# Queries and keys of the mLSTM groups and of two attention groups turned by VectorE and through DRAM

## The reference, cut to what matters

```python
scores = einsum('cbhtd,cbhsd->cbhts', q, k)              # mLSTM, times exp(gate matrix), masked
h      = scores_gated @ v / max(|row sum|, exp(-m))
s      = einsum('bshd,bmhd->bhsm', q, mk) * Dh**-0.5     # attention to the memory
out    = softmax(s) @ mv                                 # and the same, with bias, in the band
```

## Time and profile before

| | us |
|---|---|
| median of 3 runs (2137.60 to 2139.51) | 2139.01 |
| the profiled execution, its own time | 2139.0 |
| its span, first to last instruction | 2137.4 |
| TensorE busy | 2118.9 |
| VectorE busy | 1312.0 |
| ScalarE busy | 1108.1 |
| mean granted clock of TensorE, share of full | 0.997 |

### The profile page before, as it was taken

One profiled execution on the slowest core, in us unless ns is written; L12 is line 12 of the kernel. 1 busy time (PEld: TensorE's weight loads), 2 busy tenths in 40 slices (PEclk: granted clock), 3 DMA queues, 4 the chain that ended last, 5 costly groups with the idle time before them and its releaser, 6 DMA issues.

```text
span 2137.4 us, 29849 instructions
## 1 busy us (share of the span) xinstructions
PE 2118.9 (99%) x10852; PEld 1753.3 (82%) x10852; DVE 1312.0 (61%) x1745; ACT 1108.1 (52%) x1468; POOL 156.2 (7%) x256
## 2 busy tenths in 40 slices
PE   9999999999999999999999999999999999999998
PEld 7888888888888787888878888888888788888886
DVE  6456556464553877787776565566546845567467
ACT  6554545454444848474755454445444544545453
POOL 7000000000000100000010000100001211000012
PEclk9999999999999999999999999999999999999999
DMA  9866566666565555454556765755658567555654
GB/s 337 269 182 214 172 213 195 199 198 217 179 206 184 148 157 169 143 173 139 177 144 220 254 185 170 226 146 170 193 181 302 181 204 193 167 162 182 200 178 159
DMA packets 211584, 411.00 MB, mean 192 GB/s; under 512 B 14096, under 2 KB 31009, under 8 KB 211070
## 3 DMA queue, kind: packets, MB, share of 16 engines
q1 hardware_dynamic: 199440, 369.94, 55.7%
q0 software_dynamic: 9712, 30.98, 4.6%
q10 hardware_dynamic: 2304, 8.39, 1.1%
HBM read 395.19 MB, written 14.07 MB: 191 GB/s over the span
## 4 chain that ended last, share of the span: by engine, by line
PE 85%; DVE 6%; ACT 4%; issue 4%; DMA 1%; DVEq 0%; ACTq 0%; SPq 0%
PE stream_psum L663 26%; PE stream_psum L665 25%; PE stream_psum L664 25%; ACT work L1101 2%; PE heads_psum L633 2%; DVE w_low L1531 2%; ACT w_high L1101 2%; DVE work L1717 1%; PE heads_psum L1018 1%; PE heads_psum L981 1%; PE heads_psum L962 1%; DMA w_raw<-in_w_mem_kv 1%; PE heads_psum L784 0%; ACT L1101 0%; DVE work L1783 0%
## 5 line engine op out<-in xcount | busy, mean ns | idle before, releaser
L1531 DVE TENSOR_TENSOR w_low<-w_raw,w_high 128x1024 fp32r<-128x1024 f32 x688 | 829.7, 1224 | 641.0 <-ACT w_high L1101 639.0
L1101 ACT ACTIVATE w_high<-w_raw 128x1024 fp32r<-128x1024 f32 x688 | 711.1, 1057 | 465.9 <-PE stream_psum L665 387.1
L663 PE MATMUL stream_psum<-w_high,x_high 128*128 128x512 f32 x1856 | 739.7, 399 | 0.2
L665 PE MATMUL stream_psum<-w_high,x_low 128*128 128x512 f32 x1856 | 724.6, 390 | 0.0
L664 PE MATMUL stream_psum<-w_low,x_high 128*128 128x512 f32 x1856 | 723.8, 390 | 0.0
L663 PEld LDWEIGHTS stream_psum<-w_high,x_high 128*128 128x128 f32 x1856 | 349.1, 188 | 74.2 <-issue 2.2
L665 PEld LDWEIGHTS stream_psum<-w_high,x_low 128*128 128x128 f32 x1856 | 348.7, 188 | 73.3
L664 PEld LDWEIGHTS stream_psum<-w_low,x_high 128*128 128x128 f32 x1856 | 349.2, 188 | 69.8 <-issue 1.9
L663 PE MATMUL stream_psum<-w_high,y_high 128*128 128x512 f32 x896 | 354.0, 395 | 3.1 <-DVE y_low L1990 3.1
L665 PE MATMUL stream_psum<-w_high,y_low 128*128 128x512 f32 x896 | 350.3, 391 | 0.0
L664 PE MATMUL stream_psum<-w_low,y_high 128*128 128x512 f32 x896 | 350.2, 391 | 0.0
(11 more groups left out here) (321 smaller groups left out, 1269.1 us busy)
## 6 DMA issues: line engine op xcount, KB each, us to landing
w_raw<-in_w_in SPq DMA_DIRECT2D x528, 512.0 KB, 4.4
w_raw<-in_w_out SPq DMA_DIRECT2D x128, 512.0 KB, 4.9
w_raw<-in_w_mem_kv SPq DMA_DIRECT2D x32, 512.0 KB, 5.4
turned_scratch<-work POOLq DMA_DIRECT2D x40, 128.0 KB, 3.4
work<-turned_scratch POOLq DMA_DIRECT2D x10, 512.0 KB, 5.6
work<-rows_scratch POOLq DMA_DIRECT2D x8, 512.0 KB, 5.9
proj<-in_mem_t SPq DMA_DIRECT2D x8, 256.0 KB, 7.0
work<-in_x_t SPq DMA_DIRECT2D x4, 512.0 KB, 6.7
```

The lines of the kernel that those rows point to most:

```text
L663: pe.matmul(acc, hi[:, k, sl(m)], w, start=first, stop=False)
L665: return pe.matmul(acc, lo[:, k, sl(m)], w, start=False, stop=final)
L1101: return act.activation(dst, src, func, **kw)
L1531: tt(WL[:, c % RING, :], RAW[:, c % RING, :], WH[:, c % RING, :].bitcast(F32), ALU.subtract).then_inc(lo_done, 1)
```

## The change

`ml` (all four groups), `attend` of kind `m` and the first of kind `a` in each layer no longer use TensorE's transposes for queries and keys. VectorE turns them in step 2 straight from `proj` (two instructions for `ml`, where queries and keys of two heads are one tile, four for attention), GpSimd stores and loads them through DRAM (`keys_across`, one or two tiles, with a second scratch tensor), and ScalarE (and VectorE for the keys of attention) copies them to the places where they lay before. The last attention group of a layer keeps its code under the name `b`. The delta groups' value and key turns come one step later. The steps move:

| | TensorE | ScalarE | VectorE |
|---|---|---|---|
| `ml` scores, copies of q and k, product `p` | 5 to 12 | 2 to 13 | 5 to 16 |
| `ml` product with values, `expw` | 9 to 16 | 5 to 16 | |
| `ml` outputs | | 28 to 39 | 30 to 41 |
| attention `m` and `a`: scores, copies | 4 to 22 | 2 to 20 | 2 to 20 |
| attention: weights turned, values | 10, 12 to 28, 30 | 10 to 28 | 10 to 28 |
| `dn`: values turned, keys turned | 8, 23 to 9, 24 | | |

The diff, cut to its core: GpSimd's helpers and their two uses, TensorE's `ml` and `dn`, ScalarE's `ml`, VectorE's `ml` and `attend`. ScalarE's `attend` gets the same wait at step 20 and four copies of the queries.

```diff
+            def store_turned(i, at, stored):
+                for a in range(4):
+                    pool.dma_start(bass.AP(turned_d[i].tensor, a * S, [[U, QUART], [QUART * U, 4], [1, S]]),
+                                   wk(at)[sl(a, QUART), :].rearrange("p (c r) -> p c r", c=4)).then_inc(stored, 16)
+            def keys_across(n, at, to):
+                both = len(at)
+                for i in range(both):
+                    store_turned(i, at[i], keys_out)
+                wait_alone(pool, keys_out, n * 64 + 64 * both)
+                for i in range(both):
+                    pool.dma_start(wk(to[i]), turned_d[i]).then_inc(keys_in, 16)
...
             with pool.Fori(1, 4) as g:
+                wait_alone(pool, *done(ML_V, "turned_qk", g - 1))
+                keys_across(g - 1, (4,), (5,))
                 wait_alone(pool, *done(ML_V, "arg", g - 1))
...
+                pool.wait_ge(*done(AT_V["m"], "turned_qk", l))
+                keys_across(4 + 4 * l, (2, 3), (4, 5))
                 wait_alone(pool, rel_s, l * 2 + 2)
...
             def ml(g):
                 after_side(pe, g)
-                pe.wait_ge(evac, 8 * g + (2 * (E_ML + 4)))
-                for i, n in enumerate("qk"):
-                    for h in range(2):
-                        for m in range(M):
-                            last = tr(H[:, i, h * S + m * P:h * S + (m + 1) * P], PR[:, m, i * S + h * P:i * S + (h + 1) * P])
-                    last.then_inc(*signal(ML_PE, n))
-                yield from gap(3)
+                yield from gap(10)
                 q, k, w = wk(0, 512), wk(0.5, 512), wk(2, 768)
                 pe.wait_ge(*done(ML_ACT, "k", g))
...
-                yield from gap(6)
+                yield from gap(7)
                 pe.wait_ge(*done(DN_V, "conv133", g))
                 project(2, 0).then_inc(*signal(DN_PE, "v"))
-                yield from gap(9)
+                yield from gap(8)
...
-                yield from gap(6)
+                yield from gap(7)
                 pe.wait_ge(*done(DN_V, "nk", g))
...
-                act.wait_ge(*done(ML_PE, "q", g))
-                f(wk(0, 512), bank(0), ACT.Copy, scale=float(P) ** -0.5).then_inc(*signal(ML_ACT, "q"))
-                act.wait_ge(*done(ML_PE, "k", g))
-                f(wk(0.5, 512), bank(1), ACT.Copy).then_inc(*signal(ML_ACT, "k"))
+                yield from gap(11)
+                wait_alone(act, keys_in, g * 16 + 16)
+                for i, n in enumerate("qk"):
+                    for h in range(2):
+                        last = f(wk(i / 2 + h / 4, S).rearrange("p (m a t) -> p m a t", m=M, a=4), by_features(5)[:, 2 * i + h], ACT.Copy, scale=1.0 if i else float(P) ** -0.5)
+                    last.then_inc(*signal(ML_ACT, n))
                 yield from gap(3)
...
+                dve.wait_ge(evac, 8 * g + (2 * (E_ML + 1)))
+                turn(PR[:, :, 0:NBLK], 4).then_inc(*signal(ML_V, "turned_qk"))
+                yield
                 dve.wait_ge(rows_in, g * 16 + 16)
...
-                yield from gap(3)
+                yield from gap(13)
                 dve.wait_ge(*done(ML_ACT, "expw", g))
...
+                    turn(PR[:, :, 0:NBLK], 2)
+                    turn(wk(9, 2 * U).rearrange("p (m n) -> p m n", m=M)[:, :, 0:NBLK] if full else PR[:, :, NBLK:2 * NBLK], 3).then_inc(*signal(AT_V[kind], "turned_qk"))
+                    yield
...
+                if kind != "b":
+                    yield from gap(17)
+                    dve.wait_ge(keys_in, 16 * (4 + 4 * l + 2 * max(0, i - 1) + 2))
+                    for h in range(4):
+                        last = dve.tensor_copy(wk(1 + h / 4, S).rearrange("p (m a t) -> p m a t", m=M, a=4), by_features(5)[:, h])
+                    last.then_inc(*signal(AT_V[kind], "k"))
                 yield from gap(3)
                 dve.wait_ge(*done(steps, "scores", n))
```

More of the change, by code:

```diff
@@ L92, in build @@
     rel_d = nc.dram_tensor("rel_scratch", (A_H, COPIES, BIASW), F32, kind="Internal").ap()
-    turned_d = nc.dram_tensor("turned_scratch", (P, U), F32, kind="Internal").ap()
+    turned_d = [nc.dram_tensor(f"turned_scratch{i}", (P, U), F32, kind="Internal").ap() for i in range(2)]
     memt_d = [nc.dram_tensor(f"mem_{n}_scratch", (P, KT, S), F32, kind="Internal").ap() for n in ("high", "low")]
@@ L590, in _ @@
                                    bass.AP(rel_d.tensor, P - 1 - p, [[BIASW - 1, COPIES], [COPIES * BIASW, A_H], [1, S]])).then_inc(rel_bw, 16)
-                for i in range(2):
-                    pool.wait_ge(*done(AT_V["a"], "turned", 2 * l + i))
+                pool.wait_ge(*done(AT_V["a"], "turned_qk", l))
+                keys_across(6 + 4 * l, (2, 3), (4, 5))
+                for i, kind in enumerate("ab"):
+                    pool.wait_ge(*done(AT_V[kind], "turned", l))
                     across(5 + 3 * l + i, 8, 7)
@@ L826, in dn @@
                 last.then_inc(*signal(DN_PE, "k0t"))
-                yield from gap(2)
+                yield
                 def quarters(at, left, right):
@@ L942, in attend @@
                     pe.wait_ge(kv_in, (q - 8) * 16 + 64)
-                    ksrc = wk(9, 2 * U).rearrange("p (m n) -> p m n", m=M)
-                    vsrc = ksrc[:, :, NBLK:]
-                else:
-                    ksrc, vsrc = PR[:, :, NBLK:2 * NBLK], PR[:, :, 2 * NBLK:3 * NBLK]
-                for name, src, b0 in (("k", ksrc, 0), ("q", PR, 2)):
-                    for h in range(4):
-                        for m in range(M):
-                            last = tr(H[:, b0 + h // 2, (h % 2) * S + m * P:(h % 2) * S + (m + 1) * P], src[:, m, sl(h)])
-                    last.then_inc(*signal(steps, name))
+                    vsrc = wk(9, 2 * U).rearrange("p (m n) -> p m n", m=M)[:, :, NBLK:]
+                else:
+                    vsrc = PR[:, :, 2 * NBLK:3 * NBLK]
+                if kind == "b":
+                    for name, src, b0 in (("k", PR[:, :, NBLK:], 0), ("q", PR, 2)):
+                        for h in range(4):
+                            for m in range(M):
+                                last = tr(H[:, b0 + h // 2, (h % 2) * S + m * P:(h % 2) * S + (m + 1) * P], src[:, m, sl(h)])
+                        last.then_inc(*signal(steps, name))
+                else:
+                    yield from gap(18)
                 yield from gap(2)
@@ L1330, in attend @@
                 f(wk(8).rearrange("p (m n) -> p m n", m=M), PR[:, :, sl(zslot, NBLK)], ACT.Tanh, scale=0.5).then_inc(*signal(act_s, "tz"))
-                act.wait_ge(*done(steps, "q", n))
-                f(wk(0), bank(2, 2), ACT.Copy, scale=float(P) ** -0.5).then_inc(*signal(act_s, "q"))
+                l, i = divmod(q - 8, 4)
+                if kind == "b":
+                    act.wait_ge(*done(steps, "q", n))
+                    f(wk(0), bank(2, 2), ACT.Copy, scale=float(P) ** -0.5).then_inc(*signal(act_s, "q"))
+                else:
+                    yield from gap(18)
+                    act.wait_ge(keys_in, 16 * (4 + 4 * l + 2 * max(0, i - 1) + 2))
+                    for h in range(4):
+                        last = f(wk(h / 4, S).rearrange("p (m a t) -> p m a t", m=M, a=4), by_features(4)[:, h], ACT.Copy, scale=float(P) ** -0.5)
+                    last.then_inc(*signal(act_s, "q"))
                 yield from gap(4)
@@ L1903, in attend @@
                 dve.wait_ge(*done(AT_V[kind], "fg", n))
-                turn(7, 8).then_inc(*signal(AT_V[kind], "turned"))
+                turn(wk(7).rearrange("p (m n) -> p m n", m=M), 8).then_inc(*signal(AT_V[kind], "turned"))
                 yield from gap(13)
```

65 lines of the change are left out of this document (37 added, 28 removed).

## The result

The changed kernel takes 2175.13 us (median of 4 runs, 2168.26 to 2178.67), against 2139.26 for the kernel before; the ratio is 1.0166, 95% interval 1.0153 to 1.0179. The profiled execution took 2174.71 us with a span of 2173.1. Forecast were 2173.9 us and a range of 2150 to 2187.

What follows compares the result with a forecast made beforehand. TensorE, busy 99% of the span, was taken as the bound. From 2139.0 us: -9.8 transposes, -4.6 delta turns, +15.8 scores, +16.2 `p`, +1.3 restarts, +16.0 clock = +34.9, giving 2173.9 us; range 2150 to 2187.

Steps and rivals of the forecast that it cites:

- The bound and the sign: TensorE, busy 99%, sets the end and new waits go onto it; slower by more than 0.2% had chance 0.92.
- Removed transposes: 96 TensorE transposes gone from four mLSTM groups (3.2 us) and four attention groups (6.6 us): 9.8 us saved.
- The delta turns: Delta groups' turns one step later: all eight TensorE waits go, saving 3.3 us plus eight restarts of 0.16, 4.6 us.
- The wait for the scores: TensorE waits in mLSTM for turned keys crossing DRAM: 4.3 us in three groups, 2.9 in the fourth, 15.8 us.
- The wait for `p`: TensorE waits at mLSTM's product with the values, behind the block's evacuation: 4.05 us four times, 16.2 us.
- The clock: TensorE's granted clock falls to half behind each of eight new stops: 2.0 us each, 16.0 us; ends 0 and 2.8.
- Rival 1: The clock holds at the new stops, as behind the gap near the end: 2157.9 us, chance 0.20.
- Rows 12: Granted clock rows: half in 8.0 to 9.0, but 1.00 right behind an idle time of 2.76 us near the end.
- Attention showed no new wait: In attention the keys have 20 steps and arrive before TensorE reaches the scores at 1517.7: counted as 0.
- The later of the forecast's two cases: Attention keys with a crossing of 15.5 us and the late start: there by 1513, leaving 4 us of room.

Runs made afterwards that it cites:

- behind_block_split: behind_block with VectorE's gate work one step later, behind the next weight split; 2128.95 us, ratio 0.9959 to the kernel before.
- attention_only: The kernel before with the attention part of the change alone; 2132.6 us, ratio 0.9972.
- delta_only: The kernel before with only the delta value turns and key turns one step later; 2138.94 us, ratio 1.0001.
- retimed: The changed kernel with p_sooner and scores_later together and VectorE's gate work one step later, behind the next split; 2145.17 us, ratio 1.0027 to the kernel before.
- p_sooner: The changed kernel with ScalarE's exp and VectorE's mask and product one step sooner, ahead of the block's evacuation; 2151.5 us, ratio 1.0049 to the kernel before.
- scores_later: The changed kernel with the mLSTM scores two half chunks later on TensorE, product with the values unmoved; 2158.7 us, ratio 1.0097 to the kernel before.
- fill_both: fill_p with 8 more useless matmuls per mLSTM group before the wait for the scores; 2162.13 us, ratio 1.0114 to the kernel before.
- retimed_ssq: retimed with the delta groups' norm product that waits for the expanded keys one step later; 2144.65 us, ratio 1.0031 to the kernel before.
- fill_p: The changed kernel with 16 useless matmuls on TensorE before its wait for `p` in each mLSTM group; 2165.1 us, ratio 1.0121 to the kernel before.
- behind_block: The changed kernel with mLSTM scores and product with the values four half chunks later, `p` unmoved; 2131.16 us, ratio 0.9965 to the kernel before.
- both_moves: retimed without its gate work edit, so p_sooner and scores_later together on the changed kernel; 2135.3 us, ratio 0.9986 to the kernel before.

## Why the prediction was right, and where it wasn't

**The bound and the sign.** TensorE set the end, and what it newly waited for went onto it. The cost lies where the forecast put it, at L791 and L800, four times each.

**Removed transposes.** Forecast 9.8 us. The mLSTM share was 3.2: from a row ahead of the groups (85.78 before, 85.26 in behind_block_split) to the first delta group (693.24 and 689.82), where no wait is left, the distance shrank by 2.9. The attention share was 6.6; attention_only gives 6.0 (3.6 to 8.1 by its interval), and the distances of the changed kernel 7.0.

**The delta turns: wrong.** The step was that both waits go for 4.6 us and that "TensorE needs its next result (`ke`) two steps later, which covers that". The waits and restarts went, but a wait of 0.75 for `ke` came, and delta_only measured no change. The forecast asked whether the turned keys would reach VectorE in time, and they do, 4.5 us early. It didn't ask when TensorE would come to `ke` once its own stops were gone: about 0.9 us sooner, while VectorE ends `ke` at the same distance as before (41.72 and 41.75 us behind the group's first turn).

**The wait for the scores: mechanism right, size too large.** Forecast 15.8 us (4.3 three times, 2.9), measured 9.1 (1.92, 2.44, 2.72, 1.99). In the first group 0.8 of the difference is the crossing, 12.1 us instead of 13.2, and the copies' start with it; 1.6 is TensorE's arrival, 168.0 instead of 166.4. Of this 1.04 is the stop at 160.91 that the forecast lacked (0.88 and a restart), and 0.3 had come in ahead of the groups (86.08 against 85.78).

**The stop for `w_low`: missed.** 3.6 us in all, three of them 0.88. The forecast counted the turn as VectorE's work with room to spare (61% busy), but its 1.30 us stand with the gate work's 3.4 ahead of a split that TensorE was about to need. With the gate work behind that split, in retimed, the three stops of 0.88 are gone. The idle share of the whole span says nothing on one place in the queue.

**The wait for `p`: right.** Forecast 4.05 each and 16.2 together, measured 3.86 to 3.92 and 15.5. The chain, read from the rows of another block, held to 0.2 us. p_sooner and scores_later show the cause, the end of the block.

**The clock: right, a little large.** Forecast 2.0 us for each of eight stops, measured 13.6 in all, and fill_both returned 11 to 13 us of the time with the clock. That the sum is near is partly luck: 2.0 was a choice between 0 and 2.8, and the eight stops cost 0 (twice), 1.7 (three times), 2.5, 3.0 and 3.0. Rival 1, that the clock holds, was true of the stops of 2.44 and 1.99 us only. The row that spoke for it was read too short. Rows 12 show the clock at 1.00 in the microsecond behind the gap of 2.76 us; in the next one it falls:

```profile
2131.00:2132.00 1.00, 0.88 (x3) 0.19 (x1) 0.95 (x2) 0.00 (x0) 0.00 (x0) 0.60 0.39 156
```

It is 0.50 after that. So this gap, with the thin work behind it, didn't show that one of such length is let pass.

**The sum.** Forecast +34.9, measured +35.9. That it is closer than its parts is luck: the scores (6.7 too much), `p` (0.7) and the clock (2.4) stand against the delta turns (4.6 too little), the split (3.6) and the restarts of its seven stops (1.1). These corrections give +34.4; the last 1.5 us have no item. Attention showed no new wait, as forecast. The later of the forecast's two cases for it was added up too short: 1492.6 + 2.6 + 18.3 + 1.4 is 1514.9, not 1513, so the room would have been 3 us and not 4.

## What to carry to other kernels

A turn that goes through DRAM takes 10 to 15.5 us here from engine to engine, and it pays only where its reader can be put further away than the longest crossing; once that was so, the 96 fewer transposes were worth 9.9 us (2138.8 to 2128.95). Whether a step stands ahead of or behind a block's evacuation decides more than one or two steps of distance: read on every engine what is queued in front of it. Before a wait is taken out, follow its chain to the next result that the same engine needs, and ask what the stop had been hiding. TensorE comes sooner to everything behind a stop that is gone, and three times here (the delta turns, the split in retimed, `ke` in retimed_ssq) it met another wait.

## What I had not expected of the hardware

- A stop of TensorE has a price in clock that comes in few sizes. Of 26 stops of 1.9 to 3.9 us for the scores or `p` in the profiled executions of the changed kernel, p_sooner, scores_later, fill_p, retimed and retimed_ssq, six cost nothing, sixteen 1.4 to 1.7 us, and four 2.5 to 3.0 (the stop for `p` in the first group of the changed kernel, both stops of its third, one of 3.14 us in retimed_ssq). The six that cost nothing were 1.99 to 2.45 us long, but the length doesn't tell which: 2.26 us cost 1.6 in retimed's third group and nothing in fill_p's fourth. What decides I have not tested. For a sum over several stops, the mean per stop was 1.7 us in the changed kernel (13.6 over 8), 1.65 in p_sooner and scores_later, and 0.9 to 1.6 in the other three.
- Kernels with such stops also scatter more from execution to execution: 2168.26 to 2178.67 us for the changed kernel, 2143.55 to 2153.68 for p_sooner, against 2130.87 to 2131.43 for behind_block, which has none. That the price of the stops is what varies is likely, but only one execution of each was profiled.
- Matmuls of no use in a wait made the kernel faster, 24 in each group for 11 to 13 us in all.
- Moving work of 3.4 us on VectorE by one step went with a crossing through DRAM, which that work doesn't touch, that was 0.7 to 1.7 us longer in three groups and 2.9 us shorter in the fourth (retimed against both_moves).
